# Longer runs for an expert stream: gate/up weights in two transfers instead of four, down weights in one instead of two

## The reference, cut to what matters

```python
logits = (xt @ w_router + b_router)            # 256 tokens, 32 experts
top_v, top_e = lax.top_k(logits, TOP_K)        # TOP_K = 4
gates = jax.nn.softmax(top_v, axis=-1)
...
h = xb @ w_gu[e] + b_gu[e]                     # 1024 -> 2048
h_glu = jnp.minimum(h[:, :D_EXPERT], SWIGLU_LIMIT)
h_lin = jnp.clip(h[:, D_EXPERT:], -SWIGLU_LIMIT, SWIGLU_LIMIT)
act = h_glu * jax.nn.sigmoid(SWIGLU_ALPHA * h_glu) * (h_lin + 1.0)
return act @ w_dn[e] + b_dn[e]                 # 1024 -> 1024
```

## Time and profile before

| | |
|---|---|
| median of 3 runs | 1043.01 us (1040.63 to 1043.75) |
| the profiled execution's own time | 1045.26 us |
| its span, first to last instruction | 1043.3 us |
| TensorE busy, share of the span | 834.9 us, 80% |
| VectorE busy | 242.2 us, 23% |
| ScalarE busy | 72.6 us, 7% |
| mean granted clock of TensorE | 0.929 |
| read from HBM | 421.30 MB, 405 GB/s over the span |

### The profile page before, as it was taken

The page is one execution under the profiler, slowest core; times in us unless marked ns, Lnnn a source line. Parts: engine busy times, 40 slices in busy tenths (PEclk is TensorE's granted clock), DMA queues, the critical chain, the costliest instruction groups (busy, mean ns, idle before and its releaser), DMA issues.

```text
span 1043.3 us, 20077 instructions
## 1 busy us (share of the span) xinstructions
PE 834.9 (80%) x8423; PEld 361.2 (35%) x8424; DVE 242.2 (23%) x666; ACT 72.6 (7%) x171; POOL 6.1 (1%) x23
## 2 busy tenths in 40 slices
PE   9999879699668999996689977566866777966864
PEld 8885533244113433431133322111322322411321
DVE  3561712122112222221122211111111211211114
ACT  1300100000000000000000000000000000000000
POOL 1000000000000000000000000000000000000000
PEclk9999989899888999998899998877998998988987
DMA  9987597999999999999999999999999999999995
GB/s 326 412 326 311 218 430 329 427 420 422 428 431 408 423 416 432 427 428 430 427 429 429 427 430 426 430 428 428 430 428 427 431 427 428 417 428 431 427 427 207
DMA packets 39705, 422.62 MB, mean 405 GB/s; under 512 B 5852, under 2 KB 8328, under 8 KB 15240
## 3 DMA queue, kind: packets, MB, share of 16 engines
q1 hardware_dynamic: 37416, 421.96, 96.3%
q10 hardware_dynamic: 2272, 0.41, 0.2%
HBM read 421.30 MB, written 1.05 MB: 405 GB/s over the span
## 4 chain that ended last, share of the span: by engine, by line
DMA 51%; PE 40%; DVE 6%; issue 2%; SPq 0%; ACT 0%; DVEq 0%; POOL 0%; POOLq 0%
DMA dn_buf<-in_w_down_dram 51%; PE ps L815 14%; PE ps L843 13%; PE ps L683 7%; PE ps L711 3%; PE ps L809 2%; DVE act_t L643 1%; DVE lin L641 1%; DVE lin L638 1%; DVE glu L635 1%; DVE lin L636 1%; PE ps L666 0%; PE ps L698 0%; PE ps L730 0%; PE ps L671 0%
## 5 line engine op out<-in xcount | busy, mean ns | idle before, releaser
L815 PE MATMUL ps<-gu_buf,rows_t 128*32 128x512 f32 x2944 | 377.8, 658 | 117.5 <-DMA gu_buf<-in_w_gate_up_dram 117.5
L815 PEld LDWEIGHTS ps<-gu_buf,rows_t 128*32 128x32 f32 x2944 | 95.8, 116 | 390.4 <-issue 204.9
L843 PE MATMUL ps<-dn_buf,act_t 128*32 128x256 f32 x2912 | 177.1, 389 | 50.6 <-DMA dn_buf<-in_w_down_dram 42.9
L635 DVE TENSOR_SCALAR glu<-ps 128x256 f32<-128x256 f32 x46 | 19.5, 425 | 644.8 <-PE ps L815 644.8
L843 PEld LDWEIGHTS ps<-dn_buf,act_t 128*32 128x32 f32 x2912 | 90.1, 111 | 123.5 <-DMA dn_buf<-in_w_down_dram 56.9
L809 PE MATMUL ps<-turned,bias_sel 128*32 128x512 f32 x368 | 54.7, 668 | 22.4 <-issue 22.4
L683 PE MATMUL ps<-turned,gu_buf 128*128 128x256 f32 x320 | 69.6, 379 | 0.0
L683 PEld LDWEIGHTS ps<-turned,gu_buf 128*128 128x128 f32 x320 | 60.6, 190 | 8.4 <-issue 0.2
L397 ACT ACTIVATE sig<-glu 128x256 f32<-128x256 f32 x46 | 19.2, 417 | 563.4 <-DVE glu L635 563.4
L773 PE MATMUL ps<-xs,onehot 128*32 128x256 f32 x752 | 53.3, 404 | 0.0
L785 PE MATMUL ps<-mix,back 32*128 32x256 f32 x736 | 52.7, 400 | 0.5 <-ACT mix L401 0.5
(11 more groups left out here) (162 smaller groups left out, 239.1 us busy)
## 6 DMA issues: line engine op xcount, KB each, us to landing
gu_buf<-in_w_gate_up_dram SPq DMA_DIRECT2D x128, 2048.0 KB, 30.0
dn_buf<-in_w_down_dram SPq DMA_DIRECT2D x63, 2048.0 KB, 15.3
gu_buf<-in_w_in_dram SPq DMA_DIRECT2D x4, 2048.0 KB, 16.8
gu_buf<-in_w_out_dram SPq DMA_DIRECT2D x2, 2048.0 KB, 14.2
gu_buf<-in_w_in_dram SPq DMA_DIRECT2D x2, 1024.0 KB, 6.4
xs<-in_x_dram SPq DMA_DIRECT2D x2, 512.0 KB, 3.8
late<-in_ln_g_dram SPq DMA_DIRECT2D x2, 512.0 KB, 23.5
late<-in_ln_b_dram SPq DMA_DIRECT2D x2, 512.0 KB, 25.4
```

Of the source, the lines that this page charges most:

```text
L635: V.tensor_scalar(glu[:], half(HB, 0), SWIGLU_LIMIT, None, ALU.min).then_inc(S["glu_ok"], 1)
L815: ins = T.matmul(ps[SLOTS * j:SLOTS * (j + 1), HB, :], rows_t[:, k, :], gu_buf[:, b, k, :].rearrange("p (two n) -> p two n", two=2)[:, :, ...
L843: ins = T.matmul(ps[SLOTS * j:SLOTS * (j + 1), YB, 0:QF], act_t[:, DK * m + q, :], weights[q][:, QF * j:QF * (j + 1)], start=(m == 0 and q ...
```

## The change

From expert 4 on the gate/up weights come in two transfers of 4 MB (32 KB in each partition) instead of four of 2 MB, and from expert 3 on the down weights come in one transfer of 4 MB instead of two. SyncE waits once for each: for a gate/up half until the later of its two chunks has been used (`gu_used[1]`, `gu_used[3]`), for the down weights until TensorE has finished the whole down product of all blocks of the expert before (`y_ps`). TensorE waits for a gate/up half before the first of the half's two chunks, and for the whole of the down weights before the first down matmul. The last pair of experts (30 and 31) keeps its down weights in two transfers with a wait for each. The matmuls, their order and their number stay as they are; the chunk-wise `gu_used` and `dn_used` increments stay too. For experts 2 and 3 the gate/up weights still come in four transfers, but TensorE waits for them by halves.

```diff
-                                 ...[:, GRUN * c:GRUN * (c + 1)]).then_inc(gu_in[b][c], 16)
+                                 ...[:, GRUN * c:GRUN * (c + 1)]).then_inc(gu_in[b][c | 1], 16)
+            def stream_gu_halves(e, b):
+                used = blocks_before(e - 1)
+                for c in (1, 3):
+                    sp.wait_ge(gu_used[c], used)
+                    sp.dma_start(gu_buf[:, b, GK * (c - 1):GK * (c + 1), :].rearrange("p k n -> p (k n)"),
+                                 gu_src[bass.ds(e, 1)].rearrange("o p r -> p (o r)")[:, GRUN * (c - 1):GRUN * (c + 1)]).then_inc(gu_in[b][c], 16)
             def stream_dn(e):
+                sp.wait_ge(S["y_ps"], blocks_before(e))
+                sp.dma_start(dn_buf[:].rearrange("p q n -> p (q n)"),
+                             dn_src[bass.ds(e, 1)].rearrange("o p r -> p (o r)")).then_inc(dn_in[1], 16)
+
+            def stream_dn_parts(e):
                 used = blocks_before(e)
                 for c in range(DC):
-                    stream_dn_chunk(e, c, used)
+                    stream_dn_chunk(e, c, used, dn_in[c])
...
-            with sp.Fori(2, E // 2) as pair:
+            with sp.Fori(2, E // 2 - 1) as pair:
                 stream_dn(pair * 2 - 1)
-                stream_gu(pair * 2, 0)
+                stream_gu_halves(pair * 2, 0)
                 stream_dn(pair * 2)
-                stream_gu(pair * 2 + 1, 1)
-            stream_dn(E - 1)
+                stream_gu_halves(pair * 2 + 1, 1)
+            stream_dn(E - 3)
+            stream_gu_halves(E - 2, 0)
+            stream_dn_parts(E - 2)
+            stream_gu_halves(E - 1, 1)
+            stream_dn_parts(E - 1)
...
                 for c in range(GC):
-                    pe.wait_ge(gu_in[b][c], loads)
+                    if not halves or c % 2 == 0:
+                        pe.wait_ge(gu_in[b][c | 1 if halves else c], loads)
...
                 pe.wait_ge(S["act_t_sb"], now)
+                if whole:
+                    pe.wait_ge(down[1][0], down[1][1])
                 for m in range(DC):
...
-            def pair_of_experts(pair):
+            def pair_of_experts(pair, parts):
                 for b in range(2):
                     e = pair * 2 + b
-                    expert(e, b, (pair + 1) * 16, [down_at(0, e * 16), down_at(1, (e + 1) * 16)])
+                    whole = (e + 1) * 16
+                    down = [down_at(0, (b + 3) * 16), down_at(1, whole)] if parts else [down_at(0, 32), down_at(1, whole)]
+                    expert(e, b, True, (pair + 2) * 16, down, not parts)
```

More of the change, by code:

```diff
@@ L269, in stream_gu @@
                     sp.dma_start(gu_chunk(b, c),
-                                 gu_src[bass.ds(e, 1)].rearrange("o p r -> p (o r)")[:, GRUN * c:GRUN * (c + 1)]).then_inc(gu_in[b][c], 16)
-            def stream_dn_chunk(e, c, used):
+                                 gu_src[bass.ds(e, 1)].rearrange("o p r -> p (o r)")[:, GRUN * c:GRUN * (c + 1)]).then_inc(gu_in[b][c | 1], 16)
+            def stream_gu_halves(e, b):
[4 more added lines that the diff above has]
+                                 gu_src[bass.ds(e, 1)].rearrange("o p r -> p (o r)")[:, GRUN * (c - 1):GRUN * (c + 1)]).then_inc(gu_in[b][c], 16)
@@ L273, in stream_dn_chunk @@
+            def stream_dn_chunk(e, c, used, landed):
                 sp.wait_ge(dn_used[c], used)
-                sp.dma_start(dn_chunk(c), dn_src[bass.ds(e, 1)].rearrange("o p r -> p (o r)")[:, DRUN * c:DRUN * (c + 1)]).then_inc(dn_in[c], 16)
+                sp.dma_start(dn_chunk(c), dn_src[bass.ds(e, 1)].rearrange("o p r -> p (o r)")[:, DRUN * c:DRUN * (c + 1)]).then_inc(landed, 16)
             def stream_dn(e):
+                sp.wait_ge(S["y_ps"], blocks_before(e))
+                sp.dma_start(dn_buf[:].rearrange("p q n -> p (q n)"),
+                             dn_src[bass.ds(e, 1)].rearrange("o p r -> p (o r)")).then_inc(dn_in[1], 16)
@@ L277, in stream_dn @@
+            def stream_dn_parts(e):
                 used = blocks_before(e)
                 for c in range(DC):
-                    stream_dn_chunk(e, c, used)
+                    stream_dn_chunk(e, c, used, dn_in[c])
             stream_gu(2, 0)
             after_0 = blocks_before(1)
-            stream_dn_chunk(1, 1, after_0)
-            stream_dn_chunk(2, 0, after_0)
-            stream_dn_chunk(2, 1, blocks_before(2))
+            stream_dn_chunk(1, 1, after_0, dn_in[1])
+            stream_dn_chunk(2, 0, after_0, dn_in[0])
@@ L288, in _ @@
+            stream_dn_chunk(2, 1, blocks_before(2), dn_in[1])
             stream_gu(3, 1)
-            with sp.Fori(2, E // 2) as pair:
+            with sp.Fori(2, E // 2 - 1) as pair:
                 stream_dn(pair * 2 - 1)
-                stream_gu(pair * 2, 0)
+                stream_gu_halves(pair * 2, 0)
                 stream_dn(pair * 2)
-                stream_gu(pair * 2 + 1, 1)
-            stream_dn(E - 1)
+                stream_gu_halves(pair * 2 + 1, 1)
+            stream_dn(E - 3)
@@ L803, in turn_gates, with expert_block @@
                 ins.then_inc(S["gates_t_ps"], 1)
-            def expert_block(prior, now, b, loads, down, first=False):
+            def expert_block(prior, now, b, halves, loads, down, whole=False, first=False):
                 pe.wait_ge(S["sel_bias"], now)
@@ L849, in down_at, with expert @@
                 return dn_in[m], count, [dn_buf[:, DK * m + j, :] for j in range(DK)]
-            def expert(e, b, loads, down):
+            def expert(e, b, halves, loads, down, whole=False):
                 first = pe.value_load(bounds[0:1, bass.ds(e, 1)], min_val=1, max_val=MAXB - 1)
@@ L854, in expert @@
                 with pe.Fori(first, end) as g:
-                    expert_block(g, g + 1, b, loads, down)
+                    expert_block(g, g + 1, b, halves, loads, down, whole)
             down_0 = [down_at(m, 16) for m in range(DC)]
-            expert_block(0, 1, 0, 16, down_0, first=True)
+            expert_block(0, 1, 0, False, 16, down_0, first=True)
             pe.wait_ge(S["bounds_ok"], 1)
@@ L863, in _ @@
                 with pe.Fori(1, end) as g:
-                    expert_block(g, g + 1, 0, 16, down_0)
-            expert(1, 1, 16, [(S["extra_in"], 16 * GROUPS, dn_extra), down_at(1, 32)])
-            def pair_of_experts(pair):
+                    expert_block(g, g + 1, 0, False, 16, down_0)
+            expert(1, 1, False, 16, [(S["extra_in"], 16 * GROUPS, dn_extra), down_at(1, 32)])
+            def pair_of_experts(pair, parts):
                 for b in range(2):
                     e = pair * 2 + b
-                    expert(e, b, (pair + 1) * 16, [down_at(0, e * 16), down_at(1, (e + 1) * 16)])
+                    whole = (e + 1) * 16
+                    down = [down_at(0, (b + 3) * 16), down_at(1, whole)] if parts else [down_at(0, 32), down_at(1, whole)]
+                    expert(e, b, True, (pair + 2) * 16, down, not parts)
             with pe.Fori(1, E // 2 - 1) as pair:
-                pair_of_experts(pair)
+                pair_of_experts(pair, False)
             pe.wait_ge(S["bdn_in"], 16 * GROUPS)
@@ L879, in _ @@
             with pe.Fori(E // 2 - 1, E // 2) as pair:
-                pair_of_experts(pair)
+                pair_of_experts(pair, True)
             n_blocks = pe.value_load(bounds[0:1, E:E + 1], min_val=1, max_val=MAXB)
```

## The result

The changed kernel takes 1056.2 us (1053.8 to 1057.0, 4 runs), the kernel before 1043.4 us (1040.6 to 1043.8) beside it. The ratio is 1.0133, with a 95% interval of 1.0116 to 1.0149: 12.8 us slower, where 12.2 had been forecast. The profiled execution of the changed kernel took 1053.8 us (span 1051.8), so between the two profiled executions the difference is only 8.5 us.

A forecast was written before the change was run, and what follows sets the result against it. The weight stream was taken to set the end, TensorE fitting behind it. Terms 9.2 + 0.4 + 2.4 - 3.2 + 2.9 + 0.5 = +12.2 us took the profiled 1045.26 to 1057.5, predicted median 1055, range 1038 to 1082.

The forecast's parts named there:

- Part 1: Weight stream: longer runs save 9.5 ns each per engine, 0.23 us a cycle (29.37 to 29.14), 6.3 us over the kernel.
- The upper end I gave: Weight stream: largest gain from merged runs if the per-packet cost vanished altogether, 1.2% of the stream, about 10 us.
- Part 2: Two-block experts: down issue moves from T + 14.35 to T + 17.83 (T: down weights landed); cycle 30.14, 0.77 over 29.37.
- the restart cost I chose: DMA queue run dry after a late down issue: 2.6 us lost at restart, taken from between 2.2 and 4.8.
- a lead of 3.55: Expert 3's down issue at 216.67, 3.55 us before the queue's end: read as costing no loss.
- Part 3: TensorE's longer waits for data: one more two-block expert among 14, 21, 24, 26 starts at low clock, +2.9 us; end +0.5.
- Expert 7: Two-block expert starting at low clock: second down issue moves from T + 19.0 to T + 20.7, +0.4 us after its present loss.
- the end: Kernel's end: last gate/up half has 32 matmuls behind it, not 16, so activation may come later: +0.5 us (0 to 1.5).
- 1: Rival for the weight stream: transfers restart within the lead, so only the gain stays: 1037 us; chance 0.22.
- 5: Rival for the DMA packets: 32 KB runs stay 16 KB packets, gain gone and losses stay: about 1061 us; chance 0.05.
- 4: Rival for the down transfers: every queue restart costs 4.8 us, like the one at 336: 29 more, 1084 us; chance 0.11.
- 3: Rival for TensorE: the clock decides; cold starts in 14, 21, 24, 26 give 1064 us, in each of twelve 1084; chance 0.14.

The follow-up runs named there:

- gu_halves: Changed kernel with down weights back in two transfers, issued and waited for by chunk, so only the gate/up merging remains: 1036.9 us, ratio 0.9950 to the kernel before.
- after_1block: Changed kernel with one block for every expert, tokens beyond 32 left out: 1033.7 us, against 1040.9 for the kernel before with one block.
- gu_pairs: Changed kernel with down weights by chunk and gate/up chunks paired 0,2 and 1,3, giving large transfers with separate 16 KB runs: 1040.4 us, ratio 0.9981 to before.
- wait_whole: Kernel before, but TensorE waits for both down chunks before the first down matmul (experts 2 to 29), issues still by chunk: 1054.2 us, ratio 1.0122.
- issue_late: Kernel before, but both down transfers are issued after the whole down product while TensorE waits by chunk: 1050.2 us, ratio 1.0082.
- dn_whole: Changed kernel with gate/up back in four transfers and a wait for each, so only the down merging remains: 1064.8 us, ratio 1.0240 to the kernel before.
- after_2block: Changed kernel with two blocks for every expert, a third left out: 1120.9 us, against 1084.5 for the kernel before with two blocks.

## Why the prediction was right, point by point

- **Part 1, the gain.** Shown: one-block cycles 29.14 (29.14 forecast), gu_halves 29.22, after_1block 7.2 us. gu_pairs shows that it hangs on runs, as the 9.5 ns per run had it. The upper end I gave, about 10 us if the cost vanished, was mis-worked: 83 x 16 x 9.5 ns is 12.6. Nothing rested on it.
- **Part 2, release.** Shown: T + 17.9 for 17.83. The lead of 1.5 us was too short, and the restart cost I chose, 2.6, is what was measured: the ten full-clock two-block cycles of experts 4, 7, 8, 10, 11, 15, 16, 21, 24 and 26 average 30.21 us, and 30.21 - 17.9 - 9.7 = 2.6. By the 2.0 of the Trainium skill (DMA: Bandwidth & Descriptors, Anatomy of one DMA), which is given there for transfers issued by GpSimd while SyncE issues these, they would have been 29.6, an estimate; here the measurement decides.
- **What I read wrongly in part 2.** From the one transfer issued at 216.67 I took a lead of 3.55 for safe. wait_whole and issue_late show 0 to 1.8 us at 3.4. It did not enter the sum, because the changed kernel has such a lead only at expert 29, and its cycle there (30.79) is no longer than before (30.92). I had overlooked that one: in the kernel before, expert 29 issued at T + 14.35, a lead of 5.2 us, and the landing was still 1.5 us late. TensorE's down products after the two landings, and the issue:

```profile
967.84 1.93 PE L843 MATMUL ps<-dn_buf,act_t 128*32 128x256 f32 x32 [2.96 <-DMA dn_buf<-in_w_down_dram]
...
998.76 1.93 PE L843 MATMUL ps<-dn_buf,act_t 128*32 128x256 f32 x32 [1.12 <-DMA dn_buf<-in_w_down_dram]
```

```profile
982.19 2.06 SPq L274 DMA_DIRECT2D dn_buf<-in_w_down_dram  x2
```

- **Part 3, the clock.** The term of +2.9 for one of experts 14, 21, 24, 26 has the right mechanism, and was mis-sized and partly misplaced. In the profiled execution experts 9 and 14 begin low, at +1.7 each. Expert 14 is one of the four; expert 9 follows a two-block expert, which I had called safe. The two together, 3.4, come near 2.9 by chance. The price is 5.35 - 3.66 = 1.7 because the clock is back up by the end of the product (mean 0.68 over it), whereas at 318.76 us in the earlier trace rows it stayed low for 5.9 us. The page of the Trainium skill on the clock (TensorE: Matmul & The Clock Gate, on oscillation) tells of a kernel with waits for data in which every burst of matmuls after such a wait starts cold; here 3 of 14 down products of two-block experts did in the changed kernel, 7 of 14 in dn_whole.
- **Expert 7.** I counted +0.4 above the others, on top of a stall that the profiled execution already had. It came out 1.7 us shorter than before (30.21 for 31.9), because it started at full clock and the old stall was chance: the cycles of gu_pairs, with the same release times as before, have none. The spans differ by 8.5 us and the medians by 12.8, because the profiled execution of before stood 1.9 us above its median and that of the changed kernel 2.4 below. The old stall can account for the 1.9; where the 2.4 comes from is not shown.
- **Sum, from one profile to the other.** Fourteen two-block cycles together +12.5 us (12.0 forecast for the release, 2.9 for the clock), fourteen one-block cycles -3.2 (-3.2), expert 3's landing 0.8 earlier, the end 0.0 (+0.5). That is 8.5 where 12.2 was forecast from one profile to the other. So the mechanism and the size of its terms held, but that the medians lie 12.8 apart, only 0.6 from the forecast, is partly luck.
- **The rivals.** 1 falls with every two-block cycle, 5 with the packets. 4 falls too: the thirteen down transfers that restarted the queue in the changed kernel landed 12.1 to 12.4 us after their issue, a restart of 2.4 to 2.7 us, and none came near 4.8. 3 names a real cost, at a smaller rate and a smaller price.

Left open: what makes the same lead of 3.4 us cost nothing in one place and 1 us or more in another, what cost 1.5 us at expert 29 with a lead of 5.2, and why a wait of 2.07 us ahead of the down product was followed by the low clock at some landings and not at others.

## What to carry to other kernels

When a stream of weights sets the time, look at what each transfer's issue waits for, and how far ahead of the queue's end that comes: here a lead of 1.5 us or less in place of 2.2 to 5.4, in 13 of 32 experts, outweighed a rate that was 0.8% better everywhere. Merge transfers where the buffer is released early anyway (the double-buffered gate/up, 5.6 us gained), and keep them fine where the release decides (the single down buffer). Count the cases with the longest hold (two blocks), not the average one.

## What the runs showed of the hardware

- A run's fixed cost is the same from 2 KB to 64 KB, about 9.5 ns per DMA engine: 387, 408 and 428 GB/s at 2, 4 and 16 KB, cycles of 29.37, 29.22 and 29.14 as runs were merged. Two separate 16 KB runs in one 4 MB transfer gained nothing.
- A queue need not be empty by the issue order to lose time: with 3.4 us of transfers still ahead the next landing came up to 1.8 us late (wait_whole, expert 15). Once the lead was 1.5 us or less, 4 MB landed 12.1 to 12.4 us after the issue in the changed kernel, where a full queue moves them in 9.7.
- TensorE's clock fell in a stage in which it was busy 91% of the time (after_2block, 640.29 of 700 us). Six down products of that stage began low, after waits of 1.7 to 2.0 us, and each took 5.2 to 5.4 us instead of 3.66; other products began at full clock after waits as long (2.07 us at expert 13 of the changed kernel).
